# Attention's half of an output projection between the steps of a recurrence, and P·V with V stationary

## The reference

```python
x = x + 0.5 * swiglu(rmsnorm(x, ffn1_norm), ...)             # D_MODEL 2048, D_FF 5632, SEQ 256
h = rmsnorm(x, mix_norm)
hq, hf, hi, hg, nq, nkc, ... = split(h @ w_in)
o_hg  = hgrn2_mix(hq, hf, hi, hg, ...)                       # gated linear recurrence, 8 heads of 128
o_nsa = nsa_mix(rope(nq), ...)                               # sparse attention, 16 heads of 64
x = x + concatenate([o_hg, o_nsa], axis=-1) @ w_out          # 2048 x 2048
x = x + mem_cross_attn(rmsnorm(x, xattn_norm), rmsnorm(mem, mem_norm), ...)
x = x + 0.5 * swiglu(rmsnorm(x, ffn2_norm), ...)
return rmsnorm(x, final_norm)
```

## Time and profile before

| | |
|---|---|
| median of 3 runs (lowest, highest) | 2089.19 us (2088.74, 2089.35) |
| the profiled execution | 2089.34 us, its span 2087.5 us |
| PE busy | 2055.7 us, 98% of the span |
| DVE, ACT busy | 1118.3 us (54%), 941.8 us (45%) |
| chain that ended last | PE 96%, of it the unit matmuls of L1350 89% |
| mean granted PE clock | 0.982 of full speed |
| last unit of the input projection ends, first of the output projection starts | 1048.5 us, 1152.5 us |

### The profile page before, as it was taken

The page is one execution under the profiler, slowest core; times in us unless marked ns, Lnnn a source line. Parts: engine busy times, 40 slices in busy tenths (PEclk is TensorE's granted clock), DMA queues, the critical chain, the costliest instruction groups (busy, mean ns, idle before and its releaser), DMA issues.

```text
span 2087.5 us, 25300 instructions
## 1 busy us (share of the span) xinstructions
PE 2055.7 (98%) x9614; PEld 1713.4 (82%) x9614; DVE 1118.3 (54%) x1402; ACT 941.8 (45%) x1185; POOL 0.2 (0%) x4
## 2 busy tenths in 40 slices
PE   7999999999999999999989999999999999999997
PEld 6888888888888888788879888888888888888886
DVE  4454544454445455765684665655445454444444
ACT  5444444444444454544451554554444444444443
POOL 0000000000000000000000000000000000000000
PEclk9999999999999999999995999999999999999999
DMA  8666666666666656655510465466666666656653
GB/s 281 191 189 189 185 191 190 188 188 208 204 199 191 191 175 202 210 172 154 174 39 0 142 201 192 144 190 191 187 188 189 190 189 188 210 190 192 195 195 131
DMA packets 198822, 376.41 MB, mean 180 GB/s; under 512 B 13152, under 2 KB 19680, under 8 KB 198624
## 3 DMA queue, kind: packets, MB, share of 16 engines
q1 hardware_dynamic: 195984, 372.97, 59.1%
q10 hardware_dynamic: 2768, 2.48, 0.4%
HBM read 373.31 MB, written 2.10 MB: 180 GB/s over the span
## 4 chain that ended last, share of the span: by engine, by line
PE 96%; DVE 2%; ACT 1%; DMA 1%; issue 0%; DVEq 0%; SPq 0%; ACTq 0%
PE psum L1350 89%; PE psum L1361 2%; PE psum L1615 1%; PE psum L1569 1%; PE psum L1537 1%; PE psum L1550 0%; DVE att L1197 0%; DMA ident<-c_ident 0%; ACT w_hi L468 0%; DMA w_raw<-in_w_in 0%; DVE w_lo L838 0%; PE psum L1599 0%; PE psum L1646 0%; PE psum L1738 0%; PE psum L1516 0%
## 5 line engine op out<-in xcount | busy, mean ns | idle before, releaser
L838 DVE TENSOR_TENSOR w_lo<-w_raw,w_hi 128x1024 fp32r<-128x1024 f32 x696 | 850.8, 1224 | 894.2 <-ACT w_hi L468 892.9
L468 ACT ACTIVATE w_hi<-w_raw 128x1024 fp32r<-128x1024 f32 x696 | 736.8, 1060 | 1010.5 <-PE psum L1350 994.4
L1350 PE MATMUL psum<-w_hi,xT_hi 128*128 128x512 f32 (+1 forms) x1824 | 714.4, 392 | 11.8 <-DVE w_lo L838 8.7
L1350 PE MATMUL psum<-w_hi,xT_lo 128*128 128x512 f32 (+1 forms) x1824 | 709.4, 389 | 0.0
L1350 PE MATMUL psum<-w_lo,xT_hi 128*128 128x512 f32 (+1 forms) x1824 | 709.3, 389 | 0.0
L1350 PEld LDWEIGHTS psum<-w_hi,xT_hi 128*128 128x128 f32 x1824 | 343.7, 188 | 83.8 <-issue 10.2
L1350 PEld LDWEIGHTS psum<-w_hi,xT_lo 128*128 128x128 f32 x1824 | 343.7, 188 | 71.0
L1350 PEld LDWEIGHTS psum<-w_lo,xT_hi 128*128 128x128 f32 x1824 | 344.0, 189 | 68.8
L1350 PE MATMUL psum<-w_hi,ffT_hi 128*128 128x512 f32 x928 | 363.0, 391 | 0.0
L1350 PE MATMUL psum<-w_hi,ffT_lo 128*128 128x512 f32 x928 | 361.3, 389 | 0.0
L1350 PE MATMUL psum<-w_lo,ffT_hi 128*128 128x512 f32 x928 | 361.1, 389 | 0.0
(11 more groups left out here) (205 smaller groups left out, 677.5 us busy)
## 6 DMA issues: line engine op xcount, KB each, us to landing
w_raw<-in_g SPq DMA_DIRECT2D x176, 512.0 KB, 3.7
w_raw<-in_u SPq DMA_DIRECT2D x176, 512.0 KB, 3.7
w_raw<-in_d SPq DMA_DIRECT2D x176, 512.0 KB, 4.4
w_raw<-in_w_in SPq DMA_DIRECT2D x88, 512.0 KB, 4.4
w_raw<-in_w_out SPq DMA_DIRECT2D x32, 512.0 KB, 3.8
w_raw<-in_cw SPq DMA_DIRECT2D x8, 512.0 KB, 4.0
w_raw<-in_wk SPq DMA_DIRECT2D x8, 512.0 KB, 3.6
w_raw<-in_wq SPq DMA_DIRECT2D x8, 512.0 KB, 4.0
```

Source lines behind the costliest of these rows:

```text
L468: nc.scalar.activation(w_hi[:, slot], w_raw[:, slot], ACT.Copy).then_inc(w_hi_ready, 1)
L838: nc.vector.tensor_tensor(w_lo[:, slot], w_raw[:, slot], w_hi[:, slot].bitcast(F32), ALU.subtract)\
L1350: mm = nc.tensor.matmul(dst[:, t, 0:width], act_t, w[:, slot, kk, 0:width], start=(first and kk == 0 and n == 0), stop=(last and kk == KT_ ...
```

## The change

Five things change. The 42 units are spread over slots 0 to 31. The output projection is ordered by operand: 16 units that need only attention's output come first (`OUT_ORDER`, 4 column blocks times 4 slabs), one in each of slots 32 to 35, eight behind chosen steps of the recurrence (`HG_FILL`), one behind the cross product, two behind the recurrence's output and one behind its transposes; the 16 units of the recurrence's half follow, for column blocks 2, 3, 0, 1. The recurrence runs as a whole behind the attention loop, in banks 4 to 7. P·V has V stationary (128x64) and the transposed probabilities moving (128 columns), so that its output is already transposed; ACT takes the high part into `nsa_hi`, DVE the low part into `nsa_lo`, and two transpose batches with their `take`s go. Column blocks 0 and 1 are added to x in two parts (`x_part`). `nsa_hi` lies where the memory's raw tiles are loaded, so that load waits for the 16th unit.

```diff
-OUT_ORDER = (6, 7, 4, 5, 0, 1, 2, 3)
+OUT_ORDER = ([(n, j) for n in (0, 1) for j in (4, 5)] + [(n, j) for n in (0, 1) for j in (6, 7)]
+             + [(n, j) for n in (2, 3) for j in (4, 5, 6, 7)])
+OUT_NSA = len(OUT_ORDER)
+OUT_COLS = (2, 3, 0, 1)
+OUT_ORDER += [(n, j) for n in OUT_COLS for j in range(4)]
-SLOTS_U, SLOTS_ALL = 22, 36
+SLOTS_U, SLOTS_ALL = 32, 36
+HG_FILL = (0, 1, 2, 4, 7, 10, 13, 16)
-        hturn = [psum[:, 2 * b:2 * b + 2, :].rearrange("p b (k t) -> p (b k) t", t=SEQ) for b in range(2)]
+        hturn = [psum[:, 4 + 2 * b:6 + 2 * b, :].rearrange("p b (k t) -> p (b k) t", t=SEQ) for b in range(2)]
...
 # SP
+                if i == OUT_NSA + SLOTS:
+                    sp.wait_ge(unit_done, U_OUT + OUT_NSA)
+                    load_memt(0)
+                    load_memt(1)
...
 # ACT
+            def take_o(k):
+                t, g = k // 2, k % 2
+                act.wait_ge(pv_done, REP * (k + 1))
+                nc.scalar.activation(nsa_hi[:, 4 * g:4 * g + 4, t * P:(t + 1) * P],
+                                     psum[:, 7, :].rearrange("p (j s) -> p j s", s=P), ACT.Copy).then_inc(o_hi, 1)
...
 # DVE
-                nc.vector.tensor_copy(z_n[:, t, g * 512:(g + 1) * 512], psum[:, 7, :]).then_inc(o_taken, 1)
+                dve.wait_ge(o_hi, k + 1)
+                nc.vector.tensor_tensor(nsa_lo[g][:, :, t * P:(t + 1) * P], ..., ALU.subtract).then_inc(o_taken, 1)
+            def out_fill(n):
+                for _ in range(n):
+                    i = out_at[0]
+                    out_at[0] += 1
+                    if i < OUT_NSA and OUT_ORDER[i] in ((0, 7), (1, 7)):
+                        c = OUT_ORDER[i][0]
+                        dve.wait_ge(unit_done, U_OUT + i + 1)
+                        for t in range(NT):
+                            xc = x[:, t, c * NW:(c + 1) * NW]
+                            last = nc.vector.tensor_tensor(xc, pair[c][:, t, :], xc, ALU.add)
+                        last.then_inc(x_part, 1)
+                    step(U_OUT + i)
-            while hg_at[0] < HG_STEPS:
+            for k in range(HG_STEPS):
                 recurrence_step()
+                if k - 1 in HG_FILL:
+                    out_fill(1)
+            out_fill(2)
...
 # PE
-                        mm = nc.tensor.matmul(psum[:, 7, r * DH:(r + 1) * DH], probT[:, m % 2, (b * nk + kk) * P:(b * nk + kk + 1) * P],
-                                              z_n[:, kk, c0:c0 + DH], start=False, ...)
+                        mm = nc.tensor.matmul(psum[half, 7, (r // 2) * P:(r // 2 + 1) * P], z_n[:, kk, c0:c0 + DH],
+                                              probT[:, m % 2, (b * nk + kk) * P:(b * nk + kk + 1) * P], start=False, ...)
...
+                        if k == 0 and b == 1:
+                            pe.wait_ge(o_taken, 4)
...
-            while hg_at[0] < HG_STEPS:
+            for k in range(HG_STEPS):
                 recurrence_step()
+                if k in HG_FILL:
+                    out_fill(1)
...
-            batch(B_MIX, 0, lambda j, t: z_n[:, t, (4 + j) * P:(5 + j) * P], False)
+            out_fill(1)
...
-            batch(B_MIX + 1, 1, lambda j, t: z_n[:, t, j * P:(j + 1) * P], False)
-            pe.wait_ge(ho_gated, 1)
+            out_fill(2)
+            pe.wait_ge(mix_ready, 1)
+            for m in range(2):
+                batch(B_MIX + m, m, ...)
+            out_fill(1)
```

More of the change, by code:

```diff
@@ L34 @@
 W_NSA = C_GATE + NSA_HEADS * 3
+W_Z = (W_NSA + 63) // 64 * 64
 NEG = -1e30
@@ L645, in _ @@
             for t in range(NT):
-                last = nc.scalar.activation(gate[:, t], z_n[:, t, C_GATE:].rearrange("p (h b) -> p h b", b=3),
+                last = nc.scalar.activation(gate[:, t], z_n[:, t, C_GATE:W_NSA].rearrange("p (h b) -> p h b", b=3),
                                             ACT.Sigmoid)
@@ L727, in _ @@
                     takeT(2 * i - 4)
+                if i >= 6 and i % 4 == 2:
+                    take_o(i // 4 - 1)
                 if i < 16:
@@ L751, in _ @@
[L751 to L760, removed]
-                act.wait_ge(x_ready, 4 + n + 1)
-                squares(x, N_XA, n)
+            for t in range(NT):
+                act.wait_ge(ho_var, t + 1)
+                nc.scalar.activation(hst[:, 2, t], hst[:, 1, t], ACT.Sqrt).then_inc(ho_std, 1)
@@ new lines, in _ @@
+            out_fill(2)
+            for m in range(2):
+                take(B_MIX + m, m, mix_hi, 4 * m, V_HG + 4 * m)
+            out_fill(1)
+            for i, n in enumerate(OUT_COLS):
+                for j in range(4):
+                    out_fill(1)
+                    if j == 3 and i:
+                        take(B_XAN + i - 1, 0, xT_hi, 4 * OUT_COLS[i - 1], V_XA + 4 * OUT_COLS[i - 1])
+                    if 4 * i + j in MEMT_AT:
+                        split_mem(MEMT_AT.index(4 * i + j))
+                if i < 2:
+                    act.wait_ge(x_ready, 4 + i + 1)
+                    squares(x, N_XA, n)
@@ L1562, in values @@
                         pe.wait_ge(o_taken, k)
-                    nc.tensor.matmul(psum[:, 7, :], pcT[0:REP * N_CMP, t, g, :], v_blk[0:REP * N_CMP, g, :],
-                                     start=True, stop=False,
-                                     skip_group_check=True)
+                    for j in range(REP // 2):
+                        nc.tensor.matmul(psum[:, 7, j * P:(j + 1) * P], v_blk[0:REP * N_CMP, g, j * P:(j + 1) * P],
+                                         pcT[0:REP * N_CMP, t, g, :], start=(j == 0), stop=False,
+                                         skip_group_check=True)
+                half = slice((r % 2) * DH, (r % 2 + 1) * DH)
                 for b in range(2):
@@ L1614, in recurrence_step, with out_fill @@
                         c0 = (2 * hh + t) * (P // 2)
-                        mm = nc.tensor.matmul(psum[:, n % 4, c0:c0 + P // 2].rearrange("p (b m) -> p b m", m=m),
+                        mm = nc.tensor.matmul(psum[:, 4 + n % 4, c0:c0 + P // 2].rearrange("p (b m) -> p b m", m=m),
                                               kgT[:, h, t * P:(t + 1) * P], q_late, start=True, stop=True)
                 mm.then_inc(lv_done, 1)
+            out_at = [0]
+            def out_fill(n):
+                for _ in range(n):
+                    i = out_at[0]
+                    c, j = OUT_ORDER[i]
+                    u = U_OUT + i
+                    out_at[0] += 1
+                    if i < OUT_NSA:
+                        if j % 2 == 0:
+                            pe.wait_ge(o_taken, 3 if j == 4 else 4)
+                            if c >= 2 and j == 4:
+                                pe.wait_ge(x_part, c - 1)
+                            if c < 2 and j == 4:
+                                pe.wait_ge(z_ready, len(IN_GROUPS) - 1 + c)
+                        unit(u, u % SLOTS, nsa_hi, 2 * (j - 4), nsa_lo[j // 6], 2 * (j % 2), pair[c % 2], NW,
+                             j == 4, c < 2 and j == 7)
+                        continue
+                    if j == 0 and c < 2:
+                        pe.wait_ge(x_ready, 4 + c + 1)
+                    if c == OUT_COLS[0] and j % 2 == 0:
+                        pe.wait_ge(turn_lo, B_MIX + j // 2 + 1)
+                    unit(u, u % SLOTS, mix_hi, 2 * j, mix_lo, 2 * j, pair[c % 2], NW, c < 2 and j == 0, j == 3)
             def slot(q):
```

183 lines of the change are left out of this document (97 added, 86 removed).

## The result

The changed kernel takes 2071.09 us (median of 4 runs, 2069.76 to 2072.68) against 2088.97 (2088.63 to 2089.35). The ratio is 0.9914, with a 95% interval of 0.9902 to 0.9926. Built and timed once more beside the experiments, it came out at 2070.55 (2069.46 to 2072.99), ratio 0.9912 [0.9899, 0.9926]. So it is 18 us faster; 21 were forecast, inside the range given.

The account below looks back on a forecast made before the run. PE, busy 98% of the span, was taken to bound the kernel. Terms of -34.0, -1.7, +1.5, +4.5, +3.5 and +5.4 summed to -20.8 us, giving 2068 us, with a range of 2058 to 2076.

Parts of the forecast that it names:

- Term 1: Between input and output projection: PE's waits (7.8 us) and half-clock loss (26.2 us) come back, -34.0 us.
- rival 1: In the recurrence's levels: the clock falls, 5 us a fall, one or two falls giving 2073 to 2078 us; chance 0.20.
- Term 2: Attention's output: two transpose batches go, 2 x 0.87, -1.7 us.
- Term 3: P·V turned round in attention: +1.5 us for columns and +4.5 (32 x 0.14) for the array's changed shape.
- Term 4: Units behind small work: 23 more such changes on PE at 0.15 us each, +3.5 us.
- Term 5: New PE waits: 0.6 us at step 0, 3.5 in the levels, 1.3 for `mix_ready`, +5.4 us.
- the walk: PE and DVE followed side by side through the levels: five waits before levels four to eight, 3.5 us.
- Rival 3: At the 21st unit: loads bunch up, PE waits 3 us or more, 2073 us with following loads; chance 0.07.
- Rival 2: From step 0 to L1656: the clock falls and stays at half, losing 55 us, 2123 us; chance 0.03.
- Rival 4: In attention: P·V matmuls overlap with no drain, term 3 falls to -9.4 us, 2053 us; chance 0.05.
- Rival 5: Waits go, the clock doesn't matter, nothing is drained: 2060 us, the forecast's low end; no chance of its own.

Follow-up runs that it names:

- no_fill: The changed kernel with no unit between the recurrence's steps, the eight units standing behind the loop instead: 2093.46 us, ratio 1.0024 to the kernel before.
- no_waits: The changed kernel with both additions to x cut to one column and the masked copies of six levels cut to an eighth: 2065.67 us.
- pv_pair: The changed kernel with the P·V matmuls of a pair's two heads issued in turn to the two halves of the array, in one call: 2058.12 us.
- again: The changed kernel without an edit, timed and traced once more: 2070.55 us, ratio 0.9912 to the kernel before.
- pv_back: The changed kernel with P·V as before, probabilities stationary and V moving, its output left untransposed: 2063.27 us, 7.3 us less than the changed kernel.
- adds_mid: The changed kernel with DVE's two additions to x moved, the first behind the third level: 2069.59 us.
- tiny_adds: The changed kernel with the two additions to x in the levels cut to one column each: 2069.50 us.
- pair_mid: The changed kernel with two heads' P·V interleaved and the first addition to x moved behind the third level: 2057.61 us.
- pair_fill: The kernel with two heads' P·V interleaved, with the last unit among the steps moved forward behind the third level: 2062.68 us.

## Why the prediction came out as it did

**Term 1 held in the main.** The wait of L1563 and the other four went, and of the 59.2 us at a clock of 0.51 some 7 at half clock are left (from the windows at 0.73 and 0.59). That the units do it is shown by `no_fill`, which gives 23 us back with all else of the change standing; the full 34.0 were not tested by one run. The bound that I set, full clock throughout, was not reached, and by the prediction's own sign ("a window of the recurrence shows 0.5 to 0.9") that part of it was wrong: rival 1, "the clock falls in the levels", happened once. It did so in each trace of a kernel with units between the steps, except that of `no_waits`. It was priced at 5 us a fall and costs 3.3 here, since the level in which it falls is nearly the only one that it slows. Where it fell earlier, in `pv_pair`, two levels and a unit took 6.42 + 4.83 us, 4.9 more than at full clock. The reason given for it was right in its second half: waits stand behind the falls, and three levels in a row alone do not do it. `no_waits` shows that by its windows, and its time fits (4.9 us less than `again`; 1.5 of waits and 3.3 of clock in the changed kernel's trace make 4.8). But not each wait leads to a fall.

**Term 2** (two transpose batches, -1.7 us) was not tested by itself. Nothing speaks against it.

**Term 3 was mis-sized: 6.0 us forecast, 7.3 by `pv_back`, 8.2 by its rows.** The record on one half was right: 0.11 us by calls of four and eight, against 0.113. But P stationary has the same slope, 0.11 (0.37 for four, 0.82 for eight); its 0.84 / 8 = 0.105 was taken as a price for each record and is not one. So the 1.5 us for the columns are not there, and the whole loss is one per call. What was mis-sized is the way in and out, "32 x 0.14". The way in takes 0.10 us from the transposes ahead, as forecast in size (0.12), and the 0.02 for the way out had no row: the call itself is 0.20 us longer ahead of a unit and 0.09 ahead of the scores. TensorEngine Tiling in the Trainium skill (Overview and Key Properties) says that a change of the tiling mode drains the engine and that tiles run in parallel. The trace agrees with both: 0.32 us are lost at a call ahead of a unit, and a record costs 0.054 us in `pv_pair` where the halves alternate. Its 12.4 us of gain are not to be set against the 10.9 that the prediction put on alternating heads, since they hold 16 calls fewer as well.

**Term 4** (+3.5 us) was near. In attention a unit behind small work takes 2.87 us (1062.28 to 1065.15), where 2.90 was read. In the levels a unit and three levels take 2.83 + 5.30 = 8.13 us, where 2.90 + 3 x 1.84 = 8.42 was counted; four such runs make 1.2 us. Most of that belongs to term 1, which priced a level at full clock by one that stood alone.

**Term 5: 4.7 us measured, 5.4 forecast,** but spread otherwise. In the levels 1.5 us in two waits, not 3.5 in five: the first two came before the fourth and the fifth level, as in the walk (0.9 and 0.7 us for 1.1 and 0.8), and then DVE had caught up. At the start of the recurrence 0.4 for 0.6, `mix_ready` 1.0 for 1.3. Not foreseen at all was 1.1 us for `xT_lo` at the third batch of the x transposes (1222.52 to 1224.32 in the chain), with 0.5 and 0.2 in attention.

**Rival 3,** loads that bunch up, did not stop the 21st unit. The chain that ended last does reach the wait for `xT_lo` through a load of `w_out` that took 5.44 us (from 1214.51), where 3.7 is the median of its kind, right behind one of the memory's loads; whether the wait would go without it was not tried. **Rivals 2, 4 and 5** did not happen: units brought the clock back each time, even behind the 47 us of `no_fill`, matmuls on one half did not overlap, and the changed shape had its price.

**The sum.** In the profiled execution the span fell by 2087.5 - 2070.9 = 16.6 us, not 20.8. The fall adds 3.3, P·V 1.3 to 2.2, the waits take 0.7 off and the levels and units another 1.2: 2.7 to 3.6 for the 4.2 that were missing. Two waits in the first 40 us of the kernel (for the first `w_lo` and for `ident`), which the change does not touch, came out 0.8 longer (12.3 against 11.5). The second profile of the same kernel, with a span of 2067.7, would leave 1.0 missing only, though it has the same fall, so parts under 2 us can't be assigned by one trace. That the total came within 3 us of the forecast is partly luck: the fall and P·V missed one way, the waits and the levels the other.

## What to carry to other kernels

Where a chain of small steps leaves TensorE waiting and its clock falls, put pieces of dense work between the steps, and count the other engine's work in that stretch: here waits of 0.5 to 0.9 us were enough for a fall, and in the changed kernel the fall cost twice the waits. When an output is narrower than the array, let consecutive matmuls go to different halves. Here turning one round without that cost 7.3 us, against the 1.7 put on the two transpose batches that it saves, since each visit to the narrow shape is paid at both ends.

## What the runs showed of the hardware beyond what was expected

- The clock fell to half within a level behind waits of 0.88 and 0.66 us (one of 0.66 alone in `adds_mid` and `tiny_adds`, 0.89 in `again`, 0.46 in `pair_mid`). It stayed up behind one of 1.37 us in `pair_fill` and one of 0.66 in `pair_mid`, each among the same kind of levels; what tells them apart is open. The waits of 1.0 and 1.1 us at L1420, with units around them, left it at 1.00 too.
- The clock came back each time within one unit, 12 matmuls of 512 columns (4.64 us in the changed kernel; in `no_fill` it came back during the last of the 12). In 47 us of levels, back to back, it did not (`no_fill`, profiled run).
- A call over 64 stationary columns makes the stretch 0.32 us longer where a unit follows and 0.19 where the 64-row scores follow, with four records or with eight.
- A float32 record over 64 stationary columns costs 0.11 us where all go to one half and 0.054 where the two halves alternate; with 128 stationary and 64 moving columns it costs 0.11 as well. Sixteen records on the two halves in turn take no longer than eight on one, 1.02 us.
